# A hybrid decoder step on one core: in the prompt attention the reciprocals and factors of both query blocks are formed together, and the combinations come later

## What is computed

```python
sc = jnp.einsum('bqhcd,bkhcd->bhcqk', qi, kf) * SCALE
sc = sc - slopes[:, None, None, None] * dist
sc = jnp.where(dist >= 0, sc, -jnp.inf)
p = jax.nn.softmax(sc, axis=-1)
a = p[:, :, 0] - lam * p[:, :, 1]
return jnp.einsum('bhqk,bkhv->bqhv', a, vf)
```

## Time and profile before

| | us |
|---|---|
| median of three runs | 2944.46 |
| lowest, highest | 2944.05, 2945.97 |
| profiled execution | 2946.57 |
| its span in the trace | 2944.9 |

### The profile page before, as it was taken

How to read it: one execution, slowest core, us unless ns; L and a number is a source line. 1 busy time by engine, 2 the same in 40 slices (tenths; PEclk the granted TensorE clock), 3 DMA queues, 4 the chain that set the end, 5 groups by cost and what they waited for, 6 DMA issues and landing times. The chain is left out here.

```text
span 2944.9 us, 45985 instructions
## 1 busy us (share of the span) xinstructions
PE 2871.5 (98%) x17242; PEld 2414.0 (82%) x17242; DVE 1800.6 (61%) x2772; ACT 1401.1 (48%) x2234; POOL 129.0 (4%) x171
## 2 busy tenths in 40 slices
PE   8999999999999999999999999999999999988998
PEld 7888888888987888888888888789999999865787
DVE  3356556465653232477677765588888888644654
ACT  4444343343332121455556454377777777533322
POOL 0000000000000000000000000100000000022211
PEclk9999999999999999999999999999999999999999
DMA  7433433435656766497988878864444444499453
GB/s 250 161 124 122 147 122 125 147 114 175 231 186 219 235 212 207 187 295 263 297 277 280 265 240 270 247 144 99 104 110 104 107 108 115 138 417 403 166 186 107
DMA packets 326493, 567.27 MB, mean 193 GB/s; under 512 B 26761, under 2 KB 205561, under 8 KB 305689
## 3 DMA queue, kind: packets, MB, share of 16 engines
q1 hardware_dynamic: 324257, 564.61, 59.5%
q0 software_dynamic: 2048, 0.14, 0.0%
HBM read 424.69 MB, written 140.70 MB: 192 GB/s over the span
## 5 line engine op out<-in xcount | busy, mean ns | idle before, releaser
L2306 ACT ACTIVATE attn_scores<-attn_scores,attn_lowest 128x1024 f32<-128x1024 f32 (+15 forms) x256 | 306.7, 1202 | 3.7 <-DVE attn_lowest L2364 3.7
L2364 DVE CUSTOM_DVE_ANT_0 attn_scores<-attn_s,region_early 128x1024 f32<-128x1024 f32 (+7 forms) x256 | 216.6, 856 | 70.3 <-PE attn_s L2247 40.1
L273 PE MATMUL pool_acc<-pool_odd_x_hi,pool_wh 128*128 128x512 f32 (+1 forms) x640 | 223.2, 349 | 0.0
L275 PE MATMUL pool_acc<-pool_odd_x_hi,pool_wl 128*128 128x512 f32 (+1 forms) x640 | 222.9, 348 | 0.0
L274 PE MATMUL pool_acc<-pool_odd_x_lo,pool_wh 128*128 128x512 f32 (+1 forms) x640 | 222.9, 348 | 0.0
L273 PE MATMUL outa_acc<-outa_w_hi,outa_g_hi 128*128 128x512 f32 x512 | 200.4, 391 | 3.3 <-DVE outa_w_lo L1276 2.5
L273 PE MATMUL pool_acc<-even_x,pool_wh 128*128 128x512 f32 x512 | 200.1, 391 | 0.0
L274 PE MATMUL outa_acc<-outa_w_lo,outa_g_hi 128*128 128x512 f32 x512 | 199.3, 389 | 0.0
L275 PE MATMUL outa_acc<-outa_w_hi,outa_g_lo 128*128 128x512 f32 x512 | 199.3, 389 | 0.0
L275 PE MATMUL pool_acc<-even_x,pool_wl 128*128 128x512 f32 x512 | 199.3, 389 | 0.0
L274 PE MATMUL pool_acc<-even_x,pool_wh 128*128 128x512 f32 x512 | 199.2, 389 | 0.0
(11 more groups left out here) (371 smaller groups left out, 6872.0 us busy)
## 6 DMA issues: line engine op xcount, KB each, us to landing
region_early<-w_fold SPq DMA_DIRECT2D x110, 1024.0 KB, 6.5
pool_wz<-in_w_in_a SPq DMA_DIRECT2D x18, 2048.0 KB, 8.2
pool_wu<-w_mix SPq DMA_DIRECT2D x16, 2048.0 KB, 7.9
hold_kq<-in_cache_k SPq DMA_DIRECT2D x64, 512.0 KB, 6.8
region_early<-in_cache_v SPq DMA_DIRECT2D x60, 512.0 KB, 6.7
w_fold<-region_early SPq DMA_DIRECT2D x32, 896.0 KB, 5.9
region_early<-gatedT SPq DMA_DIRECT2D x16, 1024.0 KB, 5.7
gatedT<-pool_gates SPq DMA_DIRECT2D x48, 256.0 KB, 2.2
```

The source lines that it names most:

```text
L273: pe.matmul(out, ah, bh, start=first, stop=False)
L275: return pe.matmul(out, al, bh, start=False, stop=last)
L2306: act.activation(part, part, ACT.Exp, scale=-1.0, bias=low[s][:, x:x + 1], accum_out=sums[s][:, i:i + 1]).then_inc(expd, 1)
L2364: dve.tensor_tensor_reduce(sc[s][:, c, a0:a0 + n], s_ps[idx % 2][:, at0:at0 + n], bias[h % 2][:, b0:b0 + n], -SCALE, low[s][:, x - 2:x - 1 ...
```

## The change

In VectorE's program `combine` is split. A new `factors(u)` waits until all four exponentials of the unit are done and until the results of the unit that used the tiles before have both been read; it then takes one reciprocal of four sums and forms both factors in one instruction (even sums times -lam times odd reciprocals). `combine(u, r)` keeps the combination alone. The order in an iteration goes from minima 0, 1, combination of the near block, minima 2, 3, combination of the far block, minima 4, 5 to minima 0, 1, 2, 3, factors, near combination, minimum 4, far combination, minimum 5. The other engines' programs stay as they are.

```diff
+            def factors(u):
+                if not 0 <= u < NU:
+                    return
+                s = u % NSC
+                dve.wait_ge(expd, 4 * u + 4)
+                if u >= NSC:
+                    dve.wait_ge(o_done, 2 * (u - NSC) + 2)
+                dve.reciprocal(inv[s][:, :], sums[s][:, :]).then_inc(seq, 1)
+                dve.wait_ge(seq, 2 * u + 1)
+                dve.scalar_tensor_tensor(out=coef[s][:, :], in0=sums[s][:, 0::2], scalar=K["neglam"][:, 0:1],
+                                         in1=inv[s][:, 1::2], op0=ALU.mult, op1=ALU.mult).then_inc(seq, 1)
+                dve.wait_ge(seq, 2 * u + 2)
+
             def combine(u, r):
                 if not 0 <= u < NU:
                     return
                 s = u % NSC
-                dve.wait_ge(expd, 4 * u + 2 * r + 2)
-                if u >= NSC:
-                    dve.wait_ge(o_done, 2 * (u - NSC) + r + 1)
-                pair = slice(2 * r, 2 * r + 2)
-                dve.reciprocal(inv[s][:, pair], sums[s][:, pair]).then_inc(seq, 1)
-                dve.wait_ge(seq, 4 * u + 2 * r + 1)
-                dve.scalar_tensor_tensor(out=coef[s][:, r:r + 1], in0=sums[s][:, 2 * r:2 * r + 1],
-                                         scalar=inv[s][:, 2 * r + 1:2 * r + 2], in1=K["neglam"][:, :],
-                                         op0=ALU.mult, op1=ALU.mult).then_inc(seq, 1)
-                dve.wait_ge(seq, 4 * u + 2 * r + 2)
                 part = span(u, r)
...
             for u in range(NU + 1):
                 reduce(u, 0)
                 reduce(u, 1)
-                combine(u - 1, 0)
                 reduce(u, 2)
                 reduce(u, 3)
+                factors(u - 1)
+                combine(u - 1, 0)
+                reduce(u, 4)
                 combine(u - 1, 1)
-                reduce(u, 4)
                 reduce(u, 5)
```

## The result

The changed kernel takes 2985.38 us (four runs, 2983.24 to 2986.74) beside 2945.22 us (four runs): 40.2 us more, a ratio of 1.0132 with a 95% interval of 1.0119 to 1.0144. The prediction said 2986.5. The profiled execution took 2985.36 us around a span of 2983.6; the span grew by 38.7 us.

What follows compares the result with a forecast made beforehand. TensorE was taken to bound the prompt attention; new waits of 34.7 and 9.8 us plus 0.3 at the end made 44.8, less 2.6 given back, +42 us on 2944.46: 2986.5 us, range 2968 to 3000.

Steps and rivals of the forecast that it cites:

- What bounds the stage: Prompt attention runs at TensorE's pace: 79.22 of 80 us are matmul, only 7.3 us are waits for VectorE and ScalarE.
- VectorE's 29 us of relief: One reciprocal and one factor operation fewer per unit, 64 x 0.45 us; worth nothing to 7.3 us on the deciding path.
- C0 and the fourth exponential: Near combination, now also waiting for the unit's fourth exponential: no wait, its reader nearly three us later, so no cost.
- near 1: Unit whose near query block has one key block; in its iteration the far transposes were to wait 1.45 us.
- C1 behind R4: Far combination moved behind minimum 4, ending after its transposes are due: 4.34 us per head, 34.7, plus 9.8 following near-length-8 units.
- S4: Score piece that minimum 4 reads, issued late by TensorE; VectorE was to idle 0.9 us for it with near length 1.
- the signs at the prediction's end: Some 30 transpose waits of about 1.4 us, smaller score-load waits, VectorE idle 0.9 us before minimum 4, clock 1.00.
- The give-back: TensorE's 2.6 us of waits for ScalarE's copies, in units now held up elsewhere, subtracted from 44.8 to give +42 us.
- The end of the stage: Last unit's near combination, today running ahead, stands between the factors and the far combination: 0.3 us added.
- The clock: Rival: granted clock also falls, 31 units with long waits 19% slower, 59 us more, 3045 us; 4%.
- That R4 would not be held by S4: Rival: minimum 4 starts right after the near combination, wait 0.54 instead of 1.45 us, 2960 us; 7%.
- VectorE's queue as the pace: Rival: small VectorE operations delay TensorE, so the shorter queue gains at most 7.3 us, 2937 us; 3%.

Runs made afterwards that it cites:

- the last experiment: The kernel before with TensorE's steps in another order for each of the eight unit sizes, VectorE and ScalarE untouched: 2935.86 us, ratio 0.9965.

## Why the prediction was right

- **What bounds the stage** held: each wait that TensorE gained lengthened its unit, and VectorE's 29 us of relief (the pair takes 0.46 us before C0, with four reciprocals at 0.17 us and two factors at 0.22) bought nothing: the kernel with C1 moved and the third wait away, which keeps all the separate reciprocals and factors (and C0 in its old place), took 2.8 us less than the changed one.
- **C0 and the fourth exponential** cost nothing where it was said: in near 1 the factors start directly behind R3, with no wait in front of them. With C1 back in front the rest of the change costs 8 us. That price was not in the prediction and is hidden in the changed kernel, where C1 has left its place in front of R4.
- **C1 behind R4**, the term that carries the sum, came out by its own steps. Waits measured as in near 1 above, from the distance between S4 and the load: 1.45 in near 1, 1.41 and 1.41 in near 2 and 8, 0.52 in near 3, 0.50, 0.42 and 0.11 in near 5, 6 and 4, against 1.45, 1.40, 1.40, 0.49, 0.49, 0.42 and 0.09. There are 23 waits of about 1.4 us, as the sum has it, and not some 30, as the signs at the prediction's end say. One step was other than walked: in near 3 R4 is held by C0 and not by S4, by 0.05 us.
- **The give-back was too small, and in another place.** I counted 2.6 us of waits for ScalarE's copies as given back; the list after still has them, 2.6 us in 8. The 12.5 us of waits without a releaser (the row stands at the last experiment) are of the same kind, and I had not followed them. Those of near 5 and 4 stayed. In near 3 and 2 of the kernel after, the far group's late start gives the copy its time: from its load to S1 it is 1.06 and 1.07 us instead of 1.41 and 1.38. Per head 0.35 + 0.31 + 0.03 + 0.04 = 0.73 us come back, 5.8 us in all.
- **The end of the stage was too small as well.** I added 0.3 us for C0. From the last S5 to the load of the last far group it took 11.92 us instead of 10.24, 1.7 more: the minima of the last unit are followed by its exponentials, and R5, behind C1, starts them late. A third term was too large: the sum takes near 1's wait eight times, but the last, 1.45 us, is followed by a stretch in which TensorE has to wait for the last unit's combination anyway (0.93 us there, 0.66 before).
- **How good the number is.** 44.8 less 5.8 plus 1.4 less 1.45 is 39.0, beside a stage that grew by 38.2 in the traces and a median that grew by 40.2; the forecast had 42. That it came within 1.1 us of the measured time is partly luck: the terms were off by 1 to 3 us each, in both directions, and the stage in the traces, with a slower start in the kernel before, came out 4 us below the forecast.
- **The rivals.** The clock stayed at 1.00 in the changed kernel's stage, also from 1910 to 1925 us, where TensorE is busy for 12.05 of 15 us (11.93 at 0.84 in the kernel before): the 0.84 did not belong to that busy share. That R4 would not be held by S4 is refuted by the two additional instructions and by the earlier S4, for the iterations that carry the loss; VectorE's queue as the pace would have made the changed kernel faster. The Trainium skill ("VectorE: DVE Perf Modes", Rules for kernel authors) advises to minimize the count of VectorE's operations. Here that was worth 24 us where the unpaired order puts them, and nothing in front of R4; the pairing alone, in the old order, was not run.

## What to carry to other kernels

Before an operation is moved past another one, look up what that other one waits for: C1 used to fill the time in which VectorE waited for S4 anyway, and behind R4 it was added to the chain from S4 to the transposes. On the engine that sets the pace, the price is the new chain's length less the distance of its two ends in that engine's order, and it can be added up, unit by unit. What an operation costs depends on the side of the wait on which it stands: an instruction of 0.38 us disappeared in the idle time in front of it (but for the 0.12 us of its own wait, below) and lengthened the chain by 0.52 us behind it. And where a list of waits names an engine, look when that engine was done: 16 of the 48 waits put down to the combination were waits for a copy.

## What the runs showed that I had not expected

A third wait in front of an instruction cost time even though its semaphore had long been reached. With two waits VectorE's minimum started 0.18 us after the end of the scores; with three, taken by a second semaphore instruction, 0.30 us after it. TensorE got all of it: with the third wait the iterations of near 8, 5, 4, 2 and 1 are each 0.11 to 0.13 us longer than in the changed kernel, and from the third iteration on it was 5.0 us. In both kernels that have it, the second semaphore instruction stands behind the one that waits for the scores; an order with the scores' wait last was not run. In this kernel the wait belonged in front of the instruction that needs it, behind the one that is on the path.
